# A conditioned hybrid decoder layer on eight cores: late modulation sums in the prefix stage, pooled product stored in pairs, loads and output projection reordered

## What is computed

```python
mod = silu(c) @ w_ada + b_ada                      # (4, 6*1024): sh1, sc1, gt1, sh2, sc2, gt2
h = rmsnorm(x, g1) * (1 + sc1) + sh1
x_rnn, y_rnn, u_pool, g_a, g_b = split(h @ w_in)   # 5 x 1024 columns
xr = causal_conv4(x_rnn)
r, i = sigmoid(block_diag(xr, w_rg_a)), sigmoid(block_diag(xr, w_rg_x))
a = exp(-8 * r * softplus(a_param));  hr_t = a_t*hr_(t-1) + sqrt(1 - a_t^2) * i_t*xr_t
branch_a = (gelu(y_rnn) * hr) @ w_branch_a
branch_b = multiscale_pool(u_pool) @ w_branch_b    # trailing means over 2, 4, 8, 16 tokens, then w_pool
x = x + gt1 * ((sigmoid(g_a)*branch_a + sigmoid(g_b)*branch_b) @ w_out)
h = rmsnorm(x, g2) * (1 + sc2) + sh2
x = x + gt2 * (relu(h @ w_up)^2 @ w_down);  out = rmsnorm(x)
```

## Time and profile before

| | |
|---|---|
| three runs | 1367.63, 1372.73, 1373.01 us (median 1372.73) |
| profiled execution | 1365.5 us, span 1364.0 us |
| spans of the eight cores | 1344.8 to 1364.0 us |
| TensorE busy | 1105.8 us, 81% of the span, 5256 matmuls |
| VectorE, ScalarE, POOL busy | 621.7, 645.5 and 286.5 us |
| ScalarE table loads | 50, 64.2 us |
| DMA | 156.72 MB, mean 115 GB/s |

### The profile page before, as it was taken

One profiled execution on the slowest core, in us unless ns is written; L12 is line 12 of the kernel. 1 busy time (PEld: TensorE's weight loads), 2 busy tenths in 40 slices (PEclk: granted clock), 3 DMA queues, 4 the chain that ended last, 5 costly groups with the idle time before them and its releaser, 6 DMA issues.

```text
span 1364.0 us, 16866 instructions; the slowest of 8 cores (1344.8 to 1364.0 us)
## 1 busy us (share of the span) xinstructions
PE 1105.8 (81%) x5256; PEld 511.9 (38%) x5256; DVE 621.7 (46%) x919; ACT 645.5 (47%) x970; POOL 286.5 (21%) x326
## 2 busy tenths in 40 slices
PE   1376858898699889749766573999999999999994
PEld 0132433354344334314222231544444444444441
DVE  5676936766627546856855523650220120031022
ACT  2286943856817724826716401576126307415500
POOL 1232331332401504532552331110000000000000
PEclk9887978988799899969779777999999999999997
DMA  9994584394652785895865268761110110110010
GB/s 290 207 179 104 98 138 147 50 142 135 84 153 69 88 242 190 83 144 159 129 104 100 85 185 280 235 202 70 62 62 1 47 62 17 31 67 26 32 62 32
DMA packets 60248, 156.72 MB, mean 115 GB/s; under 512 B 6912, under 2 KB 22656, under 8 KB 57088
## 3 DMA queue, kind: packets, MB, share of 16 engines
q1 hardware_dynamic: 35456, 120.18, 27.8%
q0 software_dynamic: 24704, 35.46, 21.8%
HBM read 165.90 MB, written 50.34 MB: 159 GB/s over the span
## 4 chain that ended last, share of the span: by engine, by line
PE 63%; DMA 12%; issue 8%; DVE 7%; ACT 4%; POOL 3%; SPq 1%; DVEq 0%; ACTq 0%; POOLq 0%
PE ps L497 61%; DMA wTb<-w_adaT 3%; DVE a L479 2%; DMA w_gx<-w_rx 2%; DMA ada<-w_adaT 2%; DMA q_g<-dv 1%; DMA wup<-q_up 1%; PE ps L573 1%; DMA w_oo<-q_wo 1%; DVE xr L479 1%; SPq L465 1%; ACT thr L471 1%; POOL t L486 1%; POOL prodA L486 1%; ACT a L471 1%
## 5 line engine op out<-in xcount | busy, mean ns | idle before, releaser
L497 PE MATMUL ps<-h2T,wup 128*128 128x512 bf16 x1024 | 222.5, 379 | 0.0
L497 PE MATMUL ps<-wdn,ff 128*128 128x512 bf16 x1024 | 221.7, 379 | 0.0
L479 DVE TENSOR_TENSOR ps<-ps,gtb 128x512 f32<-128x512 f32 x64 | 44.5, 697 | 360.6 <-PE ps L497 360.0
L479 DVE SCALAR_TENSOR_TENSOR xr<-ps,vecs,xr 128x511 f32<-128x511 f32 (+2 forms) x192 | 137.8, 745 | 44.2 <-ACT xr L471 36.1
L486 POOL TENSOR_SCALAR stat<-stat 128x1 f32<-128x1 f32 x65 | 16.7, 257 | 655.6 <-ACT junk L471 423.8
L497 PEld LDWEIGHTS ps<-wdn,ff 128*128 128x128 bf16 x1024 | 100.2, 98 | 120.8
L497 PEld LDWEIGHTS ps<-h2T,wup 128*128 128x128 bf16 x1024 | 100.1, 98 | 120.4
L471 ACT ACTIVATE junk<-x1r 128x1024 bf16<-128x1024 f32 x16 | 16.9, 1058 | 209.3 <-DVE x1r L479 209.3
L486 POOL TENSOR_TENSOR t<-t,a 128x1024 f32<-128x1024 f32 x32 | 77.2, 2419 | 180.5 <-ACT a L471 82.8
L479 DVE TENSOR_TENSOR_SCAN a<-thr,hst,t 128x512 f32<-128x512 f32 x64 | 92.4, 1484 | 34.9 <-POOL t L486 34.8
L497 PE MATMUL ps<-prodA,w_aa 128*128 128x512 bf16 x256 | 68.6, 420 | 41.9 <-POOL prodA L486 41.9
(11 more groups left out here) (115 smaller groups left out, 1565.3 us busy)
## 6 DMA issues: line engine op xcount, KB each, us to landing
wTb<-w_adaT SPq DMA_DIRECT2D x32, 512.0 KB, 6.1
xt<-xin SPq DMA_DIRECT2D x29, 512.0 KB, 6.2
ada<-w_adaT SPq DMA_DIRECT2D x16, 512.0 KB, 18.8
q_up<-w_up POOLq DMA_DIRECT2D x32, 256.0 KB, 8.1
q_dn<-w_dn POOLq DMA_DIRECT2D x32, 256.0 KB, 15.3
wup<-q_up SPq DMA_DIRECT2D x8, 1024.0 KB, 10.7
xres<-xin SPq DMA_DIRECT2D x16, 512.0 KB, 5.9
wdn<-q_dn SPq DMA_DIRECT2D x4, 2048.0 KB, 11.8
```

The costliest lines, as they stand in the source:

```text
L479: return m(**args)
L497: ins = e.matmul(ps[tok.bank][:, lo:hi], lhsT=l, rhs=r, start=(first and i == 0), stop=(last and i == n - 1))
```

## The change

1. `_over`'s old keys become `kills`: the new buffer's first writer still waits for whoever used them, but is not entered as their writer, so the parts of one buffer (wuT.0 and wuT.1, the halves of wup) no longer wait for each other through them.
2. The planner ranks by the height of a step (the longest cost from it to the end) with 10 x rank added, takes 8 for a table change instead of 0.3, keep=1 instead of 2, and models SP's and POOL's DMAs as two queues that share a wire.
3. wuT lies elsewhere and, with wpl, waits for wx.3 (the last piece of w_x) instead of wx.1; w_gb and w_bb wait for the first xt0 and xt1 loads instead of w_gr. merge_u, hTx, u(-1) and main tile 0's hT get ranks of -0.5 to -0.42.
4. mB has 4 chunks instead of 8 and is stored in pairs, 16 DMAs of 256 KB instead of 4 of 1 MB.
5. The 32 late rows are summed in the prefix stage, from main tile 0's `mix_b` on, with one buffer wTb instead of two.
6. In the output projection the residual is loaded into x1b itself (xres is gone), x1b and xn2 lie elsewhere, and the first wup and wdn loads are written after it, in the order 2, 3, 0, 1.

```diff
-    def order(self, hop=0.15, dma_gbps=0.28, keep=2):
+    def order(self, hop=0.15, dma_gbps=0.28, keep=1, tilt=10.0, swap=8.0):
+            own = s[4] + (s[7] / dma_gbps + 2.0 if s[6] is not None else 0.0)
+            height[i] = own + max([height[j] + (0.02 if steps[j][0] == s[0] else hop) for j in post[i]], default=0.0)
+        rank_of = [-height[i] + tilt * steps[i][5] for i in range(n)]
-                            rank += 0.3
+                            rank += swap
...
-        writes += self._over(writes)
+        kills = self._over(writes)
...
-            load(f"wuT.{h}", wuT[...], w_uT[...], 2.0, -6.0, eng="pool", reads=["wx.1"])
+                load(f"wuT.{h}", wuT[...], w_uT[...], 2.0, -6.0, eng="pool", reads=["wx.3"])
-                load(f"{nm}.{h}", ..., 2.0, -5.5, eng="pool", reads=["wgr"])
+                    load(f"{nm}.{h}", ..., 2.0, -5.5, eng="pool", reads=["xt0", "xt1"])
...
-            N.add("sp", dma_fn(q_mb[m], mB[:]), reads=[f"mB{c}" for c in range(8)], writes=[f"qmb{m}"], us=0.1, rank=r, sem="qmb", mb=1.0)
+                if c % 2 == 1:
+                    j = c % 4 - 1
+                    N.add("sp", dma_fn(q_mb[m, :, c - 1:c + 1, :], mB[:, j:j + 2, :]), ..., rank=r, sem=f"qmb{j}", mb=0.25)
+        def ada_late(lo, hi):
+            for j in range(lo, hi):
+                r = 0.9 + j * 0.1
+                load("wTb", wTb[:], w_adaT[2 * D + j * P:2 * D + (j + 1) * P, :], 0.5, r - 0.1)
+                dve("stt", ["wTb", "srow"], ["junk1", f"acc{16 + j}"], 1.33, r, ...)
-        def ada_late(lo, hi):
-            for j in range(lo, hi):
-                i = j % 2
-                load(f"wTb{i}", ..., 0.5, 4.1 + j * 0.07)
-                ada_acc(16 + j, wTb[i][:], f"wTb{i}", junk1[:], "junk1", 4.3 + j * 0.07)
...
             mix_b(m, ...)
+            if m == 0:
+                ada_late(0, 32)
+                ada_done()
...
-                load(f"xres{s}", xres[s][:], xin[NTOK + row:NTOK + row + P, :], 0.5, r - 0.5)
+                load(f"x1b{s}", x1b[s][:], xin[NTOK + row:NTOK + row + P, :], 0.5, r - 0.5)
-                    tok = Bank(False)
+                    tok = Bank(True)
-                    dve("tt", [tok, f"xres{s}"], [f"x1b{s}"], 0.7, r, ..., in1=xres[s][:, hs], op=ALU.add)
+                    dve("tt", [tok, f"x1b{s}"], [f"x1b{s}"], 0.7, r, ..., in1=x1b[s][:, hs], op=ALU.add)
-        UPO = [1, 2, 3, 0]
+        UPO = [2, 3, 0, 1]
```

More of the change, by code:

```diff
@@ L620, in build_nc, with load_u, load_gb @@
         reg("wu", U1, 16 * K1)
[L621 to L629, removed]
+        band = at("band", [P, 4, 144], BF16, C0 + 6400)
+        band0 = at("band0", [P, 4, 144], BF16, C0 + 7552)
+        reg("band", C0 + 6400, 1152)
+        reg("band0", C0 + 7552, 1152)
+        def load_u():
+            for h in range(2):
+                reg(f"wuT.{h}", MG + 16 * K1, 16 * K1)
+                load(f"wuT.{h}", wuT[:, 4 * h:4 * h + 4, :], w_uT[512 * h:512 * h + 512, :].rearrange("(k p) n -> p k n", p=P), 2.0, -6.0, eng="pool", reads=["wx.3"])
+                if h == 0:
+                    load(reg("wpl", D3 + 8 * K1, 4 * K1), wpl[:], w_pl.rearrange("(k p) n -> p k n", p=P), 1.0, -6.0, eng="pool", reads=["wx.3"])
         load("band", band[:], band_d, 0.3, -5.9, eng="pool")
         load("band0", band0[:], band0_d, 0.3, -5.9, eng="pool")
[L632 to L635, removed]
+        def load_gb():
+            for nm, t, src, off in (("wgb", w_gb, w_in[:, 4 * D:5 * D], D0), ("wb", w_bb, w_b, D1)):
+                for h in range(2):
+                    reg(f"{nm}.{h}", off, 16 * K1)
+                    load(f"{nm}.{h}", t[:, 4 * h:4 * h + 4, :], src[512 * h:512 * h + 512, :].rearrange("(k p) n -> p k n", p=P), 2.0, -5.5, eng="pool", reads=["xt0", "xt1"])
         def merge_u():
@@ new lines, in mix_b @@
+                dve("stt", [f"thb{i}", tok2], [f"mB{c % 4}"], 0.7, r, out=mB[:, c % 4, :], in0=thb[:, i, :], scalar=1.0, in1=bank(tok2), op0=ALU.add, op1=ALU.mult)
+                if c % 2 == 1:
+                    j = c % 4 - 1
+                    N.add("sp", dma_fn(q_mb[m, :, c - 1:c + 1, :], mB[:, j:j + 2, :]), reads=[f"mB{j}", f"mB{j + 1}"], writes=[f"qmb{m}.{c // 2}"], us=0.1, rank=r,
+                          sem=f"qmb{j}", mb=0.25)
+        wTb = at("wTb", [P, D], F32, MG + 28 * K1)
@@ L901, in build_nc @@
             load(f"h2_{i}", h2[i][:], q_h[m], 1.0, T - 1.0, reads=[f"qh{m}"])
-            load("mBin", mBin[:], q_mb[m], 1.0, T + 0.1, reads=[f"qmb{m}"])
+            load("mBin", mBin[:], q_mb[m], 1.0, T + 0.1, reads=[f"qmb{m}.{q}" for q in range(4)])
             lru(T, lambda k, i=i: h2[i][:, k, :], [f"h2_{i}"], main=m)
@@ L967, in build_nc @@
                     scale=DV(DV_GM2, c), bias=DV(DV_SH2, c))
+        upoff = [E0, U1, U2, U3]
+        wup = [at(f"wup{q}", [P, 8, D], BF16, upoff[q]) for q in range(4)]
+        wdn = [at(f"wdn{q}", [P, 8, D], BF16, D0 + q * 16 * K1) for q in range(4)]
+        UPO = [2, 3, 0, 1]
+        for q in UPO:
+            for h in range(2):
+                load(reg(f"wup{q}.{h}", upoff[q], 16 * K1), wup[q][:, :, h * 512:(h + 1) * 512], q_up[q, :, :, h * 512:(h + 1) * 512], 1.0, 10.0,
+                     reads=[f"qup{q}.{k}" for k in range(8)])
+        for q in range(2):
+            load(reg(f"wdn{q}", D0 + q * 16 * K1, 16 * K1), wdn[q][:], q_dn[q], 2.0, 10.5, reads=[f"qdn{q}.{k}" for k in range(8)])
         for q in range(2, 4):
```

120 lines of the change are left out of this document (60 added, 60 removed).

## The result

The changed kernel took 1311.5 us (median of 4 runs, 1300.1 to 1323.8) against 1372.9 us, 61 us less; the ratio, taken from those executions alone in which no die ran slow, is 0.9494, with a 95% interval of 0.9437 to 0.955, which is 69 us. Forecast were 1326 us and a gain of 46. The slowest core is set in part by the clock that it is granted, so I also use the middle core: the median of the eight cores' spans in an execution, and of that the median over executions (leaving out those over 1400 us). It is 1360 us for the kernel before and 1294 us for the changed one (ten executions, 1289.5 to 1302.6; differences of 5 us and less are therefore not told apart).

A forecast was written before the change was run, and what follows sets the result against it. Bound taken: a chain of hand-overs differing by stage (loads, VectorE's in-order queue, last LRU's tail and residual loads), no engine full before the MLP. 5 + 8 - 35 - 24 = -46 from 1372.7 gives 1326 us; range 1290 to 1372.

The forecast's parts named there:

- The start, +5: Up to T2's first conv: first conv group some 21 us later, mostly given back; T2 at 222 against 217.1; bounds -12, +21.
- the first wuT DMA waits for the last w_x piece: Start, POOL's queue: wuT held until about 62.4 us, statistics behind it, so first conv at about 69 instead of 47.90.
- T2 and T3, +8: VectorE gets 17 us of late-row sums and 11 of waits; a third reaches TensorE; bounds -25 and +28.
- rival (c): Prefix gets tighter by itself, 20 to 25 us off T2 and T3: 1302 us; chance 0.17.
- rival (d): One-buffer late rows become the chain, every short gap on the path: about 1390 us, T2 and T3 +28; chance 0.12.
- 11 us of short gaps: T2 and T3: VectorE's waits where its other work between two late-row sums is shorter than a row's load.
- the shortfalls against 6.1 us: Nine of 31 gaps between late-row sums fall short of a load's landing time: 38 us, 11 in T2 and T3.
- the 150 us slower: Late rows with one buffer, by the double-buffer rule: each of 32 sums pays its 6.1 us load; the forecast rejected it.
- Main tiles, -35: 405.5 to 757.6 us: w_oo's wait, sums' waits and clock gain, short gaps in T4 and T5 cost 17; bounds -60, -13.
- 13 us for w_oo's wait: Main tiles: 13 of TensorE's 14.9 us wait for w_oo go, as 64 matmuls now stand ahead of it.
- Output projection, -24: 757.6 to 915.1 us: residual waits 22, w_aa wait about 10, clock 4 gained; some 12 lost; bounds -40 and 0.
- At nothing: Costed at zero: matmul count, table changes, mB's paired stores, wup's independent sub-keys, last wdn piece; MLP unchanged at 449 us.

The follow-up runs named there:

- weight 12: Planner's weight of rank against height 12 for 10: changed kernel, ratio 0.958; the one with late rows back in the main tiles, ratio 0.9399.
- statistics first: Changed kernel, same order else, with the wuT loads and wpl behind hTx's two statistics on POOL: middle core 1287.4 us, ratio 0.9436.
- store late: Changed kernel, same order else, with the first q_g store issued in T5 behind the 29th late row: middle core 1282.8 us, ratio 0.94.

## Why the prediction came out as it did

**The total** lay in the range and the sign was right, but -46 against -69 is a sum in which one term had the wrong sign (the start), one came near by luck (T2 and T3, where two errors cancel), and one had in part the wrong cause (the projection).

**The start, +5, measured -7.6.** The step that failed is "the first wuT DMA waits for the last w_x piece": it waits for piece 3, which the planner now issues first, so the wait ends with the first landing (48.8 us) and not with the last. All that followed from it was as written: with piece 3 last, POOL is released at 59.9, xn stands at 63.4, the first conv at 65.2 (forecast 69) and T2 at 219.8 (forecast 222). A row of the order list that says x4 does not tell which four.

**T2 and T3, +8, measured +2.5.** This is luck. With the rows back in the main tiles T2 and T3 take 165.5 us: the other edits save 23 us against the kernel before (rival (c)'s mechanism and size), and the rows with what rides on them cost 25 (nearly rival (d)'s +28). I had put one at nothing and the other at 8. The step that failed is the price of the rows: 11 us of short gaps and 17 of work, a third of them on TensorE. Two buffers change the waits by 12 of 66 us and the end by nothing measurable, so the shortfalls against 6.1 us were the wrong sum. The Trainium skill ("Trainium Kernel Development and Optimization", Best Practices) says to double-buffer so that DMA overlaps compute. The run with two buffers shows no gain from it here, and by the measurement the change was not the 150 us slower that my estimate from that rule had it. One of the large waits is settled: 14.57 us behind the small store, which I had costed at nothing because I had not asked what becomes of q_g when its sums move ahead. The others were not taken apart; that SP stands in order behind other waits fits them, but no run shows it alone.

**Main tiles, -35, measured -29.4.** Here the mechanism held. The rows' part of my sum was -29 and -10 for waits and clock and +17 for short gaps, together -22; between the kernel with the rows back and the changed one it measures -24 (343.5 to 319.3, over two orders, so a draw is in it). The rest, 13 us for w_oo's wait, measures -5 (348.7 to 343.5). What failed is the balance with the prefix: I let the move win some 14 us (8 + 17 against 39), and in all it loses 17 to 21. Part of that is not the sums. The start and the store, each tried alone, are worth 3 to 7 and 5 to 11 us; added up they could be most of the 17, but both together were not run, and with weight 12, where the store lands sooner, the loss is no smaller. So the cost of the sums themselves in the prefix stays open, but for the 22 us that they and their waits cost in the changed kernel's order.

I had read VectorE's 62% in T2 and T3 as room. With the rows there TensorE idles 31 us more and its clock is 0.87 instead of 0.96. Rival (d), the rows as chain, is not shown: with the old planner T4 starts at 444, near its mark of 450, but VectorE waits 11.5 us for rows there, while the longest standstill comes with the small store. What I had put nowhere in the sum is the planner, which is worth 38 us with all other edits in. They stand in T2 and T3 (239.3 us against 190.9), and how much of them is the place of the store was not tried.

**Output projection, -24, measured -34.7.** By idle time it is -23.7 (58.2 to 34.4), of which the edit itself is 12 to 26, depending on the planner; the rest on core 7 is 12.7 us less busy time: 31 matmuls that now stand ahead of the first w_oo (7 us) and a higher clock (0.97 against 0.95). The wait that I had put in the middle, VectorE on xres, is small where the order differs.

**At nothing.** That the halves no longer wait for each other was costed at nothing, for wup alone. It measures 8 us, little more than a draw of the order, and what the profile shows of it is wuT's second half, issued at 83 us instead of at 49. The MLP showed no change, as forecast. mB's smaller buffer shows no wait in the changed kernel, but with the rows back VectorE waits 12.9 us once for its store, so it is not free in every order.

Not run: the new planner alone in the kernel before, and statistics first and store late together, with the rows in the prefix, which would tell the price of the sums there. What the planner's parts (heights, table price, wires) are worth one by one stays open.

## What to carry to other kernels

That an engine is busy for only part of a stage (62% here) does not make work that is moved there free. Measure such a move with the rest of the change both in and out, and measure each stage at its own places: here a better order elsewhere hid the loss, and in T2 and T3 the two cancelled to +2.5 us. When a list scheduler ranks by what lies behind a step, each edit lays a new order: hold the order fixed to price one edit, and draw two orders (here 6 us apart) before believing a difference of that size. When a computation is moved, follow its last products too: a store of 4 KB set free earlier cost 5 to 11 us.

## What the hardware showed

The q_g store moves 4 KB in 4-byte pieces. Issued at 240.8 us, with the eight q_wga casts of 256 KB under way on POOL's queue, it took 28.7 us to land, and under the old planner, also beside them, 45.2 us. While it was under way the DMA engines' busy share was 1.50 at 105 GB/s (0.63 at 150 GB/s in the same stretch without it), and 512 KB loads on the same queue took 22.7 and 23.1 us against a median of 5.3 and 6.1. It is not the store alone: beside the casts without the store two xt loads took 12.2 and 17.7 us, and behind the casts (weight 12) the store itself took 16.3 us.

Two cores of one die can be granted less of the clock than the other two. In the run with two buffers cores 2 and 3 had 0.83 and 0.81 from 700 to 860 us and the six others 0.93 to 0.95; these two ended at 1311 and 1312 us, the rest at 1284 to 1296. So medians over the cores told differences that the slowest core did not.
